# Eight more projections of a two-block transformer kernel in three reduced-precision products instead of one float32 product

## The chip, the cores and the metric

The kernel runs on one core of one Trainium2 chip. The metric is the device time of one execution in microseconds (us). The engines that matter are PE (TensorE, the matmuls), DVE (VectorE), ACT (ScalarE), POOL (GpSimd) and SP, whose queue issues the loads of the weights.

## The reference, cut to what matters

Two networks run one after the other. The first, which the change touches, has two blocks (i = 0 and 1) on 256 tokens of width 1024. All data are float32.

```python
for i in range(DEPTH):
    y = swiglu(x, ffn_w_gate[i, 0], ffn_w_up[i, 0], ffn_w_down[i, 0])
    x = layer_norm(ALPHA * x + 0.5 * y, ln_g[i, 0], ln_b[i, 0])
    y = mixer_ab(x, ...) if i % 2 == 0 else mixer_c(x, ...)    # 16 heads of 64, ends in o @ w_out
    x = layer_norm(ALPHA * x + y, ln_g[i, 1], ln_b[i, 1])
    y = memory_attn(x, mem, mem_w_q[i], mem_w_kv[i], mem_w_o[i])
    x = layer_norm(ALPHA * x + y, ln_g[i, 2], ln_b[i, 2])
    y = swiglu(x, ffn_w_gate[i, 1], ffn_w_up[i, 1], ffn_w_down[i, 1])
    x = layer_norm(ALPHA * x + 0.5 * y, ln_g[i, 3], ln_b[i, 3])

def memory_attn(h, mem, w_q, w_kv, w_o):                       # 4 heads of 256, 256 memory rows
    q = (h @ w_q).reshape(...)
    k, v = jnp.split(mem @ w_kv, 2, axis=-1)
    p = softmax(q k^T * MEM_HEAD_DIM ** -0.5)
    return (p v).reshape(B, S, D) @ w_o
```

## The kernel before, in words

Each engine runs one program, in order, and waits on semaphores that other engines raise. `Net` holds what both networks share; `First` holds the first network, with one method for each engine (`tensor`, `scalar`, `vector`, `gpsimd`).

**Weights.** Every weight matrix is streamed from memory in pieces of 128 x 2048 values (1 MB), four to a 1024 x 1024 matrix. `stream_sync` issues them in the order of `net.stream` from SP into a ring of five slots (`weight_ring`), and a piece is issued when the piece five before it has been used by PE (L308 issues weights, L291 other loads).

**Two ways to multiply.** `product` is one place for both. Without halves it is one float32 matmul (L352). With halves, weights and rows each stand as a float32r high part and a float32r low part, and `product` makes three matmuls: low rows by high weights (L349), high rows by low weights (L350), high by high (L351). The trace has two records for each float32 matmul and one for each float32r matmul, so a projection of 1024 x 1024 is 64 or 128 records of L352, or 96 or 192 of L349 to L351 together. `proj_tensor` gives rows in tokens (moving width 512, 32 products), `projT_tensor` gives them transposed (moving width 256, 64 products).

**Making halves.** For weights, `split_scalar` (ACT, L338) waits until the piece has landed and until a slot of the ring of four high halves is free, and copies the piece rounded; `split_vector` (DVE, L344) waits for that and subtracts, over the piece itself. For rows, `halves_copy` does the same from PSUM: ACT takes the high half (L455), then DVE subtracts (L458).

**Before the change** the halves are used in all feed-forward layers, the mixers' input projections and the memory query. Mixer output (`mix_out`), memory keys (`mk`), memory values (`mv`) and memory output (`mo`) of both blocks are float32.

**Attention.** `attn_tensor`, `attn_vector` and `attn_scalar` are three loops over heads, each in the fixed order of its own code. In iteration i PE does scores of head i+1 (L663), the four transposes of the probabilities of head i-1 (L673) and the values of head i-2 (L688). DVE does `top(i)` (in heads with a bias L718, then row maximum L723 and small operations up to L731 or L733), `normalise(i-1)` (to L744), and, where four heads (one in memory attention) are complete, `out(g)`, a copy of PSUM into `oT` (L749). ACT does the exponentials of head i (L777) and the copy of the transposed probabilities of head i-1 (L792). `top(i)` is what the exponentials wait for, and `normalise` what the transposes wait for. The mixer of block 0 has 16 heads, of which 8 to 15 have a window bias and a sink; that of block 1 has 16 heads with a bias, which POOL masks (L1280) after loads from memory.

**Around attention** the order of a block is: feed-forward, normalisation, transposes of x, input projections, mixer attention, `mix_out`, `mk`, `mv`, transposes of x, `mq`, memory attention, `mo`, normalisation (`ln_vector`, L822 to L836, first rows 0 to 127, then 128 to 255), transposes of x (L467), feed-forward. The normalisation after `mix_out` runs beside `mk`; that after `mo` has nothing on PE beside its second part.

## Time and profile before

| what | value |
|---|---|
| device time, median of 3 runs | 3536.83 us (3518.06 to 3536.93) |
| the profiled execution's own time | 3532.46 us |
| its span, first to last instruction | 3530.7 us |
| PE busy | 3180.4 us (90%) |
| DVE busy | 1574.4 us (45%) |
| ACT busy | 1041.6 us (30%) |
| mean granted TensorE clock | 0.938 of full |
| loads of block 1's mixer output weights (4 pieces), issue to landing, median | 9.1 us |
| the same for most other 1 MB pieces | 4.9 to 5.3 us |

All rows are from the one profiled execution. A time in front of a row of a timeline is its start in us from the start of the span. The granted clock is a share of TensorE's full clock: 1.00 is 2.4 GHz, 0.50 is 1.2 GHz. A busy time of PE overlaps with that of its neighbours, because matmuls are pipelined; the time of a stage is therefore read from start to start.

### The profile page before, as it was taken

What the parts mean: (1) busy time and instruction counts of PE and PEld (TensorE: products, weight loads), DVE (VectorE), ACT (ScalarE), POOL (GpSimd) and SP (SyncE); (2) the same over time, 40 slices, a digit from 0 to 9 for tenths busy, and PEclk for the clock granted to TensorE, in tenths of its full rate; (3) what the DMA queues carried; (4) which work ended last, traced back from release to release, by engine and by line L of the source; (5) the groups of instructions that cost most, each with busy time, mean ns of one, the idle gap of its engine ahead of it and who ended that gap; (6) DMA issues with size and microseconds to landing.
All of it is one profiled execution on the core that took longest, in us unless ns stands there. A gap on an engine that the chain in (4) does not pass through costs nothing.

```text
span 3530.7 us, 33459 instructions
## 1 busy us (share of the span) xinstructions
PE 3180.4 (90%) x14288; PEld 2381.6 (67%) x14288; DVE 1574.4 (45%) x1875; ACT 1041.6 (30%) x1220; POOL 106.7 (3%) x85
## 2 busy tenths in 40 slices
PE   8986999976989999797989799988897999999999
PEld 6873668755774768643774488445843788888887
DVE  4446234433444244426742444257433444444444
ACT  4333124323332234203110243131001343434343
POOL 0001000000011000000000000000000000000000
PEclk9998999987998999898899899997998999999999
DMA  6540435545623445353104255432032455555554
GB/s 249 171 160 11 155 131 191 183 126 148 204 84 119 160 137 181 106 178 114 40 2 156 72 180 178 145 118 73 1 124 69 143 182 183 187 181 191 174 173 149
DMA packets 249105, 487.97 MB, mean 138 GB/s; under 512 B 36318, under 2 KB 67678, under 8 KB 248574
## 3 DMA queue, kind: packets, MB, share of 16 engines
q1 hardware_dynamic: 248576, 482.17, 41.1%
q10 hardware_dynamic: 380, 3.66, 0.4%
q8 instruction: 113, 1.85, 0.2%
q14 instruction: 36, 0.29, 0.0%
HBM read 481.08 MB, written 4.69 MB: 138 GB/s over the span
## 4 chain that ended last, share of the span: by engine, by line
PE 78%; DVE 9%; DMA 5%; ACT 3%; SPq 2%; issue 1%; POOL 1%; ACTq 0%; DVEq 0%; POOLq 0%
PE psum L352 18%; PE psum L349 16%; PE psum L351 16%; PE psum L350 16%; PE psum L1861 2%; SPq L291 2%; PE psum L1937 2%; PE psum L688 2%; PE psum L467 2%; PE psum L663 2%; PE psum L1848 2%; DMA weight_ring<-in_ffn_w_gate 1%; DMA weight_ring<-in_moe_wd 1%; ACT weight_high_halves L338 1%; PE psum L549 1%
## 5 line engine op out<-in xcount | busy, mean ns | idle before, releaser
L344 DVE TENSOR_TENSOR weight_ring_low_halves<-weight_ring,weight_high_halves 128x2048 fp32r<-128x2048 f32 (+1 forms) x346 | 743.3, 2156 | 963.9 <-ACT weight_high_halves L338 963.7
L349 PE MATMUL psum<-weight_high_halves,stage_area_halves 128*128 128x512 f32 (+2 forms) x2616 | 1011.7, 387 | 60.5 <-DVE weight_ring_low_halves L344 55.5
L351 PE MATMUL psum<-weight_high_halves,stage_area_halves 128*128 128x512 f32 (+2 forms) x2616 | 1001.9, 383 | 0.0
L350 PE MATMUL psum<-weight_ring_low_halves,stage_area_halves 128*128 128x512 f32 (+2 forms) x2616 | 1001.8, 383 | 0.0
L338 ACT ACTIVATE weight_high_halves<-weight_ring 128x2048 fp32r<-128x2048 f32 (+1 forms) x346 | 622.4, 1806 | 867.3 <-PE psum L351 399.8
L352 PE MATMUL psum<-weight_ring,stage_area 128*128 128x512 f32 (+2 forms) x1600 | 674.8, 583 | 12.3 <-DMA weight_ring<-in_w_in 7.3
L349 PEld LDWEIGHTS psum<-weight_high_halves,stage_area_halves 128*128 128x128 f32 x2616 | 500.2, 191 | 158.2 <-DVE weight_ring_low_halves L344 54.2
L351 PEld LDWEIGHTS psum<-weight_high_halves,stage_area_halves 128*128 128x128 f32 x2616 | 499.4, 191 | 98.9
L350 PEld LDWEIGHTS psum<-weight_ring_low_halves,stage_area_halves 128*128 128x128 f32 x2616 | 499.2, 191 | 93.9
L352 PEld LDWEIGHTS psum<-weight_ring,stage_area 128*128 128x128 f32 x1600 | 306.0, 193 | 367.8 <-issue 366.0
L448 ACT ACTIVATE stage_area<-psum 128x512 f32<-128x512 f32 (+2 forms) x126 | 71.8, 578 | 656.9 <-PE psum L352 394.3
L455 ACT ACTIVATE stage_area_halves<-psum 128x512 fp32r<-128x512 f32 (+2 forms) x148 | 78.9, 571 | 211.5 <-PE psum L549 129.4
L498 POOL TENSOR_TENSOR small<-small,constants 128x1 f32<-128x1 f32 (+5 forms) x45 | 65.2, 1449 | 2322.2 <-DVE small L831 1292.1
L458 DVE TENSOR_TENSOR stage_area_halves<-psum,stage_area_halves 128x512 fp32r<-128x512 f32 (+2 forms) x148 | 90.5, 650 | 84.1 <-ACT stage_area_halves L455 83.2
L467 PE MATMUL psum<-constants,stage_area 128*128 128x128 f32 x272 | 42.0, 315 | 83.8 <-DVE stage_area L1485 31.7
L663 PE MATMUL psum<-stage_area 64*128 64x256 f32 (+1 forms) x288 | 88.3, 457 | 22.8 <-DVE stage_area L718 14.4
L595 ACT ACTIVATE stage_area<-psum 128x512 f32<-128x512 f32 (+2 forms) x108 | 59.9, 554 | 155.3 <-PE psum L351 155.2
L467 PEld LDWEIGHTS psum<-constants,stage_area 128*128 128x128 f32 x272 | 36.5, 163 | 95.7 <-DVE stage_area L1485 35.0
L663 PEld LDWEIGHTS psum<-stage_area 64*128 64x128 f32 (+1 forms) x288 | 55.5, 220 | 53.9 <-issue 22.2
L688 PE MATMUL psum<-stage_area 128*64 128x256 f32 (+1 forms) x288 | 83.3, 432 | 0.0
L349 PE MATMUL psum<-stage_area_halves,weight_ring_low_halves 128*128 128x256 f32 x256 | 74.4, 291 | 6.2 <-DVE stage_area_halves L458 6.2
L449 DVE COPY stage_area<-psum 128x512 f32<-128x512 f32 (+1 forms) x42 | 28.5, 678 | 115.0 <-PE psum L467 114.4
(244 smaller groups left out, 2298.9 us busy)
## 6 DMA issues: line engine op xcount, KB each, us to landing
weight_ring<-in_ffn_w_down SPq DMA_DIRECT2D x44, 1024.0 KB, 5.0
weight_ring<-in_ffn_w_gate SPq DMA_DIRECT2D x40, 1024.0 KB, 5.2
weight_ring<-in_ffn_w_up SPq DMA_DIRECT2D x40, 1024.0 KB, 5.2
weight_ring<-in_moe_wd SPq DMA_DIRECT2D x40, 1024.0 KB, 4.9
weight_ring<-in_w_in SPq DMA_DIRECT2D x36, 1024.0 KB, 5.2
weight_ring<-in_moe_wg SPq DMA_DIRECT2D x32, 1024.0 KB, 5.2
weight_ring<-in_moe_wu SPq DMA_DIRECT2D x32, 1024.0 KB, 5.2
weight_ring<-in_mem_w_kv SPq DMA_DIRECT2D x16, 1024.0 KB, 5.2
```

The source lines that it names most:

```text
L338: act.raw.activation(self.high_half(name), self.in_slot(name), ACT.Copy).then_inc(*act.mark("high_halves", ("high", name)))
L344: v.raw.tensor_tensor(self.low_half(name), self.in_slot(name), self.high_half(name), ALU.subtract).then_inc(*v.mark("low_halves", ("halves ...
L349: pe.raw.matmul(out, a[1], w[0], start=start, stop=False)
L350: pe.raw.matmul(out, a[0], w[1], start=False, stop=False)
L351: return pe.raw.matmul(out, a[0], w[0], start=False, stop=stop)
L352: return pe.raw.matmul(out, a, w, start=start, stop=stop)
L448: return eng.raw.activation(dst, src, ACT.Copy)
L455: eng.raw.activation(dst[0], src, ACT.Copy).then_inc(*eng.mark("high_half_taken", (name, "high")))
L458: eng.raw.tensor_tensor(dst[1], src, dst[0], ALU.subtract).then_inc(*self.drained(eng, bank, full, name))
L467: mm = pe.raw.transpose(self.ps[:, g["bank"], i * P:(i + 1) * P], block, self.ident)
L663: mm = pe.raw.matmul(net.ps[:, bank, m * S:(m + 1) * S], h["q"](j, m), h["k"](j), start=(j == 0), stop=(j == h["nk"] - 1))
L688: mm = pe.raw.matmul(net.ps[p0:p0 + rows, bank, ct * S:(ct + 1) * S], h["v"](part, kt), net.pT[:, i % 2, kt, :], start=(kt == 0), stop=(kt ...
```

## The change

Mixer output, memory keys, memory values and memory output of both blocks are planned with `split=True`, so that each of their 32 pieces gets a high half on ACT and a low half on DVE, and PE makes three matmuls in place of each float32 one. The attention output `oT` is written as two halves (`attn_out`: ACT, then DVE) in place of DVE's single copy. The transposed memory `memT` gets halves in each block after the mixer attention (`mem_halves`: one ACT and one DVE operation of 128 x 2048), in space that the query, the probabilities and their transposes have held until then.

The places in the two engines' orders: the four pieces of `mix_out` are split in iterations 11, 12, 13 and 14 of the mixer attention, on ACT after the copy of the transposed probabilities, on DVE at the iteration's end. The four of `mk` are split after the attention, ahead of the normalisation on DVE. Those of `mv` are split on ACT between the copies of `mk`, on DVE after the normalisation. Two pieces of `mo` are split before the memory attention, the third in its iteration 0, the fourth in iteration 1.

```diff
         self.xT_proj = (self.xT_halves[0], self.halves_part(10240, KT, S))
+        self.oT_halves = self.xT_proj
         self.ffn_hT = (self.halves_part(6144, 4, S), self.halves_part(9216, 4, S))
...
-def attn_vector(net, v, tag, heads, per_group, need_bias=()):
+def attn_out(net, eng, tag, g):
+    src = net.ps[:, 4 + g % 2, :].rearrange("p (a t) -> p a t", a=2)
+    dst = [half[:, 2 * g:2 * g + 2, :] for half in net.oT_halves]
+    net.halves_copy(eng, dst, src, 4 + g % 2, (tag, "values", g), (tag, "oT", g))
+def attn_vector(net, v, tag, heads, per_group, ahead=None):
     n = len(heads)
...
     def out(g):
+        if ahead is not None:
+            return attn_out(net, v, tag, g)
         v.wait_ge(*v.at((tag, "values", g)))
...
-def attn_scalar(net, act, tag, heads):
+        net.split_vector(v, (ahead or {}).get(i, []))
+def attn_scalar(net, act, tag, heads, per_group=4, ahead=None):
     n = len(heads)
...
-    for i in range(n + 1):
+    for i in range(n + (1 if ahead is None else 3)):
         if i < n:
             exps(i)
-        if i >= 1:
+        if 1 <= i <= n:
             turned(i - 1)
+        if ahead is None:
+            continue
+        net.split_scalar(act, ahead.get(i, []))
+        if i >= 3 and (i - 3) % per_group == per_group - 1:
+            attn_out(net, act, tag, (i - 3) // per_group)
...
         self.memT = net.part(18944, KT, S)
+        self.memT_halves = (net.halves_part(2048, KT, S), net.halves_part(8192, KT, S))
         self.mem_tok = net.part(E, MT, D)
...
                 st["ab_in"] = net.plan_proj("ab_in", ins["ab_w_in"][0], blocks(1536), KT, split=True)
-                st["mix_out"] = net.plan_proj("ab_out", ins["ab_w_out"][0], blocks(D), KT)
+                st["mix_out"] = net.plan_proj("ab_out", ins["ab_w_out"][0], blocks(D), KT, split=True)
             else:
...
                 self.load_bias(3)
-                st["mix_out"] = net.plan_proj("c_out", ins["c_w_out"][0], blocks(D), KT)
+                st["mix_out"] = net.plan_proj("c_out", ins["c_w_out"][0], blocks(D), KT, split=True)
             wkv = ins["mem_w_kv"][i]
-            st["mk"] = net.plan_proj(f"mem{i}_k", wkv[:, 0:D], blocks(D), KT)
-            st["mv"] = net.plan_proj(f"mem{i}_v", wkv[:, D:2 * D], blocks(D), KT)
+            st["mk"] = net.plan_proj(f"mem{i}_k", wkv[:, 0:D], blocks(D), KT, split=True)
+            st["mv"] = net.plan_proj(f"mem{i}_v", wkv[:, D:2 * D], blocks(D), KT, split=True)
             self.load_norm(4 * i + 2)
             st["mq"] = net.plan_proj(f"mem{i}_q", ins["mem_w_q"][i], blocks(D), KT, split=True)
-            st["mo"] = net.plan_proj(f"mem{i}_o", ins["mem_w_o"][i], blocks(D), KT)
+            st["mo"] = net.plan_proj(f"mem{i}_o", ins["mem_w_o"][i], blocks(D), KT, split=True)
             self.load_norm(4 * i + 3)
...
         net = self.net
-        oT = lambda k, m: net.oT[:, k, m * P:(m + 1) * P]
+        oT = lambda k, m: pick(net.oT_halves, k, m)
+        memT = lambda k, m: pick(self.memT_halves, k, m)
+        memT_all = lambda k: (self.memT_halves[0][:, k, :], self.memT_halves[1][:, k, :])
         xT = lambda k, m: pick(net.xT_proj, k, m)
...
-            net.projT_tensor(pe, st["mk"], lambda k: self.memT[:, k, :], range(4),
-                             [("memT", m, kg) for m in range(MT) for kg in (0, 4)])
-            net.proj_tensor(pe, st["mv"], lambda k, m: self.memT[:, k, m * P:(m + 1) * P], rot)
+            net.projT_tensor(pe, st["mk"], memT_all, range(4), [("memT_halves", i)])
+            net.proj_tensor(pe, st["mv"], memT, rot)
             net.turn_tensor(pe, self.x_turn(n + 2))
...
+    def mem_halves(self, eng, i, tag, heads):
+        high, low = self.memT_halves
+        if eng.name == "scalar":
+            eng.wait_ge(*eng.at(*[("memT", m, kg) for m in range(MT) for kg in (0, 4)], (tag, "oT", heads // 4 - 2),
+                                (tag, "pT", heads - 1), (tag, "values", heads // 4 - 1)))
+            eng.raw.activation(high, self.memT, ACT.Copy).then_inc(*eng.mark("memory_high_half", ("memT_high", i)))
+        else:
+            eng.wait_ge(*eng.at(("memT_high", i)))
+            eng.raw.tensor_tensor(low, self.memT, high, ALU.subtract).then_inc(*eng.mark("memory_halves", ("memT_halves", i)))
...
                 net.turn_copy(act, self.ab_turn())
-                attn_scalar(net, act, "ab", self.ab_heads())
+                tag, heads = "ab", self.ab_heads()
             else:
...
                 net.proj_copy(act, st["c_v"], rot, self.v_take)
-                attn_scalar(net, act, "c", self.c_heads())
-            net.projT_copy(act, st["mk"], range(4), net.kT, ["scalar"])
+                tag, heads = "c", self.c_heads()
+            out, mk, mv, mo = (st[name]["pieces"] for name in ("mix_out", "mk", "mv", "mo"))
+            attn_scalar(net, act, tag, heads, 4, {11 + j: [out[j]] for j in range(4)})
+            self.mem_halves(act, i, tag, len(heads))
+            net.split_scalar(act, mk)
+            for half in range(2):
+                net.projT_copy(act, st["mk"], range(4), net.kT, ["scalar"], range(2 * half, 2 * half + 2))
+                net.split_scalar(act, mv[2 * half:2 * half + 2])
             net.proj_copy(act, st["mv"], rot, self.v_take, [0])
...
             residual_scalar(net, act, n + 2)
-            net.projT_copy(act, st["mq"], range(4), net.qT, ["scalar"])
-            attn_scalar(net, act, f"mem{i}", self.mem_heads())
+            for half in range(2):
+                net.projT_copy(act, st["mq"], range(4), net.qT, ["scalar"], range(2 * half, 2 * half + 2))
+                net.split_scalar(act, mo[:2] if half == 0 else [])
+            attn_scalar(net, act, f"mem{i}", self.mem_heads(), 1, {0: mo[2:3], 1: mo[3:]})
             net.split_scalar(act, st["ffn1"]["gate_up"][0][:2])
...
                 net.turn_copy(v, self.ab_turn())
-                attn_vector(net, v, "ab", self.ab_heads(), 4)
+                tag, heads = "ab", self.ab_heads()
             else:
                 net.split_vector(v, st["c_k"]["pieces"] + st["c_v"]["pieces"])
-                attn_vector(net, v, "c", self.c_heads(), 4)
+                tag, heads = "c", self.c_heads()
+            out, mk, mv, mo = (st[name]["pieces"] for name in ("mix_out", "mk", "mv", "mo"))
+            attn_vector(net, v, tag, heads, 4, {11 + j: [out[j]] for j in range(4)})
+            self.mem_halves(v, i, tag, len(heads))
+            net.split_vector(v, mk)
             ln_vector(net, v, n + 1, 1.0, self.y_names(st["mix_out"]["tag"]))
+            net.split_vector(v, mv)
             net.split_vector(v, st["mq"]["pieces"][:2])
...
             net.split_vector(v, st["mq"]["pieces"][2:])
-            attn_vector(net, v, f"mem{i}", self.mem_heads(), 1)
+            net.split_vector(v, mo[:2])
+            attn_vector(net, v, f"mem{i}", self.mem_heads(), 1, {0: mo[2:3], 1: mo[3:]})
             net.split_vector(v, st["ffn1"]["gate_up"][0][:2])
...
             net.turn_copy(v, self.x_turn(n + 3))
```

## Rows read from the trace of the kernel before

**Rows 1.** The page: the chain that ended last, by engine.

```profile
PE 78%; DVE 9%; DMA 5%; ACT 3%; SPq 2%; issue 1%; POOL 1%; ACTq 0%; DVEq 0%; POOLq 0%
```

**Rows 2.** Busy time by stage: three outputs together, memory keys, query, c values, two attentions.

```profile
core 0: us, PE busy (x) PEld busy (x) DVE busy (x) ACT busy (x) POOL busy (x), PEclk, DMA share, GB/s
343.90:426.60 82.70, 82.70 (x258) 48.73 (x259) 15.53 (x18) 7.77 (x9) 3.04 (x2) 1.00 0.44 147
371.50:399.10 27.60, 27.60 (x130) 24.29 (x129) 5.52 (x8) 1.79 (x3) 1.52 (x1) 1.00 0.36 129
431.00:455.20 24.20, 24.01 (x191) 23.81 (x190) 4.49 (x2) 5.67 (x8) 0.00 (x0) 0.93 0.26 92
1030.90:1053.20 22.30, 22.30 (x99) 18.00 (x97) 4.59 (x2) 6.49 (x7) 0.00 (x0) 1.00 0.16 48
290.10:343.80 53.70, 46.21 (x192) 26.65 (x192) 37.14 (x116) 27.71 (x89) 0.00 (x0) 0.90 0.00 1
455.80:473.00 17.20, 16.07 (x80) 13.53 (x81) 9.04 (x25) 8.06 (x21) 0.00 (x0) 1.00 0.51 183
```

**Rows 3.** Groups by line and shape: the weight halves and the low half of rows.

```profile
L338 ACT ACTIVATE weight_high_halves<-weight_ring 128x2048 fp32r<-128x2048 f32 x285 | 544.8, 1919 | 695.9 <-PE psum L351 282.5 <-DMA weight_ring<-in_ffn_w_gate 154.4 <-DMA weight_ring<-in_ffn_w_down 67.9
L344 DVE TENSOR_TENSOR weight_ring_low_halves<-weight_ring,weight_high_halves 128x2048 fp32r<-128x2048 f32 x285 | 652.6, 2299 | 819.6 <-ACT weight_high_halves L338 819.5
L458 DVE TENSOR_TENSOR stage_area_halves<-psum,stage_area_halves 128x512 fp32r<-128x512 f32 x122 | 78.5, 682 | 30.3 <-ACT stage_area_halves L455 30.1
```

**Rows 4.** Timeline of block 0, head 10 of the mixer attention (start, us).

```profile
318.65 0.68 DVE L718 SCALAR_TENSOR_TENSOR stage_area<-psum,constants 128x512 f32<-128x512 f32 x1
321.35 0.35 DVE L744 TENSOR_SCALAR stage_area<-stage_area,small 128x256 f32<-128x256 f32 x1
321.76 0.66 PE L673 MATMUL psum<-constants,stage_area 128*128 128x128 f32 x4 [0.25 <-DVE stage_area L744]
322.22 0.68 DVE L718 SCALAR_TENSOR_TENSOR stage_area<-psum,constants 128x512 f32<-128x512 f32 x1
322.45 0.60 ACT L792 ACTIVATE stage_area<-psum 128x512 f32<-128x512 f32 x1 [0.44 <-PE psum L673]
```

**Rows 5.** Timeline of block 1, mixer attention, heads 10 to 15 and its end.

```profile
1090.52 2.48 SPq L308 DMA_DIRECT2D weight_ring<-in_c_w_out  x4
1098.67 0.60 ACT L792 ACTIVATE stage_area<-psum 128x512 f32<-128x512 f32 x1 [2.77 <-PE psum L673]
1102.57 0.69 DVE L718 SCALAR_TENSOR_TENSOR stage_area<-psum,stage_area 128x512 f32<-128x512 f32 x1 [2.87 <-PE psum L663]
1107.52 0.69 DVE L718 SCALAR_TENSOR_TENSOR stage_area<-psum,stage_area 128x512 f32<-128x512 f32 x1 [2.61 <-PE psum L663]
1111.63 0.69 DVE L718 SCALAR_TENSOR_TENSOR stage_area<-psum,stage_area 128x512 f32<-128x512 f32 x1 [0.47 <-PE psum L663]
1118.07 0.69 DVE L749 COPY stage_area<-psum 128x512 f32<-128x512 f32 x1 [2.85 <-PE psum L688]
```

**Rows 6.** Timeline of the memory attention of block 0.

```profile
458.73 0.47 ACT L777 ACTIVATE stage_area<-psum,small 128x256 f32<-128x256 f32 x1 [3.08 <-DVE small L733]
459.52 0.69 DVE L723 TENSOR_REDUCE small<-psum 128x2 f32<-128x512 f32 x1 [0.83 <-PE psum L663]
461.83 0.69 DVE L723 TENSOR_REDUCE small<-psum 128x2 f32<-128x512 f32 x1 [0.69 <-PE psum L663]
473.01 1.53 PE L352 MATMUL psum<-weight_ring,stage_area 128*128 128x512 f32 x3 [0.83 <-issue]
```

**Rows 7.** Timeline of block 0, end of memory output and its normalisation.

```profile
494.00 1.29 DVE L822 SCALAR_TENSOR_TENSOR x<-psum,scaled_residual 128x512 f32<-128x512 f32 x2 [1.16 <-PE psum L352]
507.10 1.97 PE L467 MATMUL psum<-constants,x 128*128 128x128 f32 x8 [5.50 <-DVE x L836]
```

**Rows 8.** Three stretches of attention, columns as in rows 2; granted clock third from last.

```profile
336.00:339.00 3.00, 1.21 (x7) 0.88 (x8) 2.42 (x12) 1.70 (x6) 0.00 (x0) 1.00 0.00 0
339.00:342.00 3.00, 3.00 (x13) 1.82 (x11) 0.09 (x1) 0.68 (x2) 0.00 (x0) 0.53 0.00 0
1104.00:1107.00 3.00, 3.00 (x8) 1.62 (x6) 0.85 (x4) 1.30 (x5) 0.00 (x0) 0.50 0.76 281
```

## The prediction

> **What bounds the kernel now.** I read the page first. PE is busy for 90% of the span, by its line in the table of times, and stands for 78% of the chain that ended last; DVE has 9% of the chain and ACT 3% [rows 1]. So matmul time taken away should come off the end nearly one for one, unless the stage in which new work is put has another bound. That is why I read the stages next. In the float32 projections PE has no gap: mixer output, memory keys and memory values together take 82.7 us, all of them busy, and memory keys alone 27.6 of 27.6. In attention that is not so. Block 0's mixer attention holds PE for less than its 53.7 us, and DVE and ACT are both well occupied there, with small operations that feed each other [rows 2]. The new splitting work goes into exactly these stages, so the timelines of attention decide, and I read those last.
>
> **What the products save.** A float32 projection takes 82.7 / 3 = 27.6 us. The shape of mixer output, memory values and memory output in three products is measured in the c values projection: 96 matmuls in 22.3 us at full clock. Each such projection saves 27.6 - 22.3 = 5.3 us. Memory keys take 27.6 us too; their shape in halves is the memory query, 24.2 us at a mean clock of 0.93. A stretch at half clock for 7% of twice the time is 3.4 us, which costs 1.7 us, so 22.5 at full clock: 5.1 us saved [rows 2]. Six of the first and two of the second: 6 x 5.3 + 2 x 5.1 = 42.0 us.
>
> The Trainium skill, FP8 and Floating Point Precision, section TensorE Precision Notes, says that true float32 takes four passes, each high or low half with each. The trace agrees with the direction but not with the ratio: three products should then take 3/4 of 27.6, 20.7 us, and the c values took 22.3 [rows 2]. By the page's ratio the saving would be 8 x 6.9 = 55 us.
>
> **What the splitting costs inside mixer attention, block 0.** Making halves of a piece is 1.92 us on ACT and then 2.30 us on DVE [rows 3]. Summed over 34 operations on each engine (32 pieces, 2 memories) that is 65 and 78 us, which both engines have free. But the order matters. In iteration i, DVE does `top(i)`, `normalise(i-1)` and then must wait for the high half that ACT makes in the same iteration; ACT makes it only after the copy of the transposed probabilities of head i-1, and this needs PE's transposes, which need `normalise(i-1)`. Nothing on ACT can run ahead, as its exponentials wait for `top(i)`. So one iteration becomes a chain. In iteration 10 DVE starts at 318.65, ends `normalise` at 321.70, PE's transposes run from 321.76 to 322.42 and ACT's copy from 322.45 to 323.05 [rows 4]. With a split behind it: high half to 324.97, low half to 327.3, and only then the next `top`. That is 8.6 us from start to start. Now it is 3.57 (318.65 to 322.22), of which DVE's copy of `oT`, which this iteration holds, is 0.6; without one it is 2.97. Iterations 11, 12 and 13 each cost 5.6 us more, 16.9 us.
>
> Iteration 14 also holds an `oT` copy. It is 3.57 us now and becomes 8.6 + 0.6 (ACT's `oT` high half behind the split) + 0.6 (DVE's, 0.68 with overlap) = 9.8: 6.2 us more. In iterations 6 and 10, without a split, DVE waits for ACT's high half of `oT`: ACT's copy ends at 323.05, 0.60 for the high half, as for that copy, and 0.68 for the low one [rows 3] give 324.3 where 322.22 stood: 2.1 us each, 4.2. At the attention's end the single copy becomes two operations in a row, 0.65 more. Sum for block 0: 16.9 + 6.2 + 4.2 + 0.65 = 27.9 us.
>
> **Block 1.** Here the iterations are longer, since the clock is at half for much of it: 4.95 us from 1102.57 to 1107.52 [rows 5], with a granted clock of 0.50 [rows 8]. More of the chain is therefore already paid. In iteration 11 ACT's copy ends at 1099.27; high and low half end at 1103.5. From there iterations 12 and 13 take 1.65 (`top`) + 0.65 (`normalise`) + 1.1 to 1.2 (transposes at half clock) + 0.6 + 1.92 + 2.30 = 8.4 us each, and iteration 14 8.4 + 1.2 = 9.6. The first three parts are read off the same kind of rows as in block 0. `top(15)` comes at 1103.5 + 8.4 + 8.4 + 9.6 = 1129.9. Now it comes at 1111.63, 7.2 us before the attention's end (its last copy ends at 1118.76). That is 18.3 us more. Iterations 6 and 10 cost some 2 each as before, the end 0.65: 23 us. The pieces themselves should have landed: they are issued between 1090.5 and 1093.0 [rows 5] and take 9.1 us in the median, so the first may come at 1099.6, beside its turn at 1099.3, and the others well before theirs.
>
> **Memory attention, twice.** Its iterations 0 and 1 each hold a split. ACT's exponentials of head 0 begin at 458.73 and take 1.0; high half to 461.7, low half to 464.0. `top(1)` now starts at 459.52, so it is 4.5 late. Then `normalise(0)` ends at 465.7, transposes 0.6, copy 0.6, high half to 468.9, low half to 471.2, and `top(2)`, now at 461.83, starts 9.3 late [rows 6]. Behind that, each of four heads has its `oT` in two steps: `normalise(3)` comes after the first, the last values wait for a bank that the second frees, and the last pair ends the stage. Walking that through gives 2.0 more: 11.3 us, 22.6 for both.
>
> **What lies outside attention.** The halves of `memT` and of `mk` run beside mixer output, whose pieces free the four high slots at 8.3, 11.1, 19.4 and 22.2 us. The last low half of `mk` ends some 28.8 us after mixer output began, ahead of its use at 33.5. It pushes the normalisation to 28.8 to 41.4 (now 21.0 to 34.0), and behind this the first low halves of `mv` end at 43.7 and 45.9, where PE wants them at 44.8 and 47.6. About 1 us of cover is left; if a load lands later, it is paid one for one. I cost this at nothing.
>
> After memory output the cover is thinner. DVE's normalisation now begins at 494.0 when PE has done the first 128 rows, 21.0 us after memory output began at 473.01; its two parts take 6.2 to 6.5 us each; PE's transposes start at 507.10, 34.1 us after that beginning [rows 6, 7]. With memory output at 22.2 us its first slot is free after 8.4 us, the piece lands 5 us later, its halves end at 17.8, which is later than the 17.0 at which PE is done with those rows, and 17.8 + 6.2 + 6.2 + 0.1 = 30.3 follows. The gain that reaches the transposes is 3.8, not 5.3: 1.5 us lost each time, 3.0 in all.
>
> **The clock.** A gap of 1.9 us on PE in this attention (busy 1.21 of 3 us) is followed by a stretch at 0.53, though PE is busy throughout it; elsewhere it stays at 0.50 for longer [rows 8]. In the changed iterations PE has 2.6 us of work in 8.6, so I expect 1.2 GHz there. What it can cost: 0.45 for each of four transposes in block 0's loop, 1.8; up to 2.5 at its end; up to 4.0 at block 1's end, which now runs at full clock; 1.7 at the start of each mixer output (what the memory query now pays), 3.4; 3 in each memory attention, 6. That is 17.7 at most, and nothing at least. I take half, 9, since the gaps recur but not each need throw the clock.
>
> **Sum.** 27.9 + 23 + 22.6 + 3.0 + 9 = 85.5 us added, 42.0 taken off: 43.5 us slower. On the profiled execution's 3532.5 us that is 3576 us. The median of the runs stands 4.4 us above this execution, so against it the forecast is 1.1% slower.
>
> **Rivals.** *The chain is absorbed, and the kernel ends faster.* If DVE did not have to wait for ACT in the attention iterations (high halves ready before DVE asks), only DVE's own 2.3 us would be added, and in part in its idle time. With the splits wholly hidden the sum is 42.0 - 3.0 - 13.5 (the `oT` pairs: 4.2 + 4 + 1.3 + 4) = 25.5 faster, 3507; with all twelve low halves paid it is 3534, about no change. The point from which it decides is a price of (42.0 - 16.5) / 12 = 2.1 us for each of twelve splits in attention; I read 4.5 to 5.6. For it speaks only that both engines have much free time [rows 2]. Against it stands the order of the code.
>
> *The products gain more.* With the page's 3/4 the saving is 55 and the time 3563. The c values' 22.3 us speak against it.
>
> *The clock stays low for longer.* If each stall leaves PE at half clock, as rows 8 show once, for the whole 17.7, and the projections behind the four attentions lose another 1.7 each, the time is 3576 + 8.7 + 6.8 = 3592.
>
> *The clock does not fall at all:* 3576 - 9 = 3567.
>
> **How the numbers follow.** The chain as worked out, 3562 to 3590: 0.60. The clock stays low for longer: 0.16. The products gain more, or several terms are each somewhat smaller, 3550 to 3565: 0.12. The chain absorbed, 3507 to 3540: 0.12. A measurement of this kernel can tell about 1%, 35 us, from no change. Slower by more than that starts at 3568 on the profiled execution's base: most of the first case and all of the second, 0.63. Within 1%: 0.32. Faster by over 1% needs even the hidden case to gain more than it can: 0.05. The range is 3545 to 3603.
>
> **What would show it.** Right: start to start of L718 in block 0 of some 8.6 us in iterations 11 to 13 against 2.97; DVE's idle time before L344 ending with ACT's L338 inside attention; block 0's mixer attention near 82 us, memory attention near 28 to 31 instead of 17.2; projections at 22.3 to 22.6 us; a granted clock near 0.5 where heads 11 to 15 run. Wrong: if L718 keeps its spacing in those iterations the chain does not exist; if memory keys or mixer output take much over 22.5 us behind their cold start, the halves come late; if PE waits at the start of memory values, the 1 us of cover was not there.

## The result, and the profile after

The changed kernel takes 3575.6 us (median of 4 runs, 3567.91 to 3578.07), the kernel before in the same session 3532.12 us (4 runs, 3518.06 to 3536.93): a ratio of 1.0126, 95% interval 1.0091 to 1.0161. The profiled execution took 3578.07 us with a span of 3576.3 us, 45.6 us more span than before.

The page of the changed kernel, the line of busy times and the chain by engine:

```profile
PE 3155.9 (88%) x14608; PEld 2419.5 (68%) x14608; DVE 1650.2 (46%) x1909; ACT 1113.1 (31%) x1270; POOL 106.7 (3%) x85
...
PE 75%; DVE 11%; DMA 5%; ACT 4%; SPq 2%; issue 2%; POOL 1%; ACTq 0%; DVEq 0%; POOLq 0%
```

PE is busy for 24.5 us less in sum and its share of the chain falls from 78% [rows 1] to 75%; DVE's rises from 9% to 11%, ACT's from 3% to 4%. The products got cheaper and the end moved to the two engines that feed the attentions.

The stretches that answer to [rows 2], in one view of busy time by stretch of the changed kernel: memory keys with mixer output ahead of it (378.0 to 422.7), memory query, the two mixer attentions, the two memory attentions.

```profile
core 0: us, PE busy (x) PEld busy (x) DVE busy (x) ACT busy (x) POOL busy (x), PEclk, DMA share, GB/s
378.00:422.70 44.70, 44.70 (x288) 40.54 (x289) 25.91 (x23) 13.99 (x10) 3.04 (x2) 1.00 0.41 141
449.20:474.30 25.10, 24.34 (x192) 24.15 (x193) 9.08 (x4) 10.06 (x10) 0.00 (x0) 0.93 0.25 91
293.30:377.90 84.60, 56.73 (x192) 31.39 (x193) 46.29 (x120) 37.91 (x98) 0.00 (x0) 0.72 0.00 1
1087.90:1175.30 87.40, 59.56 (x194) 32.30 (x193) 50.76 (x104) 38.77 (x91) 9.31 (x4) 0.69 0.28 84
474.40:505.50 31.10, 21.04 (x81) 16.41 (x81) 13.25 (x26) 12.13 (x26) 0.00 (x0) 0.84 0.28 102
1271.70:1301.50 29.80, 20.09 (x80) 15.09 (x80) 13.25 (x26) 12.13 (x26) 0.00 (x0) 0.89 0.30 106
```

Mixer output and memory keys together are 44.9 us with no gap on PE. Mixer attention of block 0 is 84.6 us long where it was 53.7, and PE is busy for 56.7 of them at a granted clock of 0.72. That is also where the length of the kernel went. Measured from the first matmul of a stage to that of the next, from both timelines:

| stage | before | after | block 1 before | block 1 after |
|---|---|---|---|---|
| mixer attention | 53.73 | 84.68 | 65.52 | 87.43 |
| mixer output | 27.54 | 22.27 | 27.54 | 22.27 |
| memory keys | 27.62 | 22.61 | 27.63 | 22.62 |
| memory values | 27.47 | 22.19 | 27.47 | 22.19 |
| transposes, memory query | 29.31 | 29.33 | 29.32 | 29.32 |
| memory attention | 17.22 | 31.18 | 17.22 | 29.84 |
| memory output to feed-forward | 35.70 | 31.80 | 35.69 | 31.98 |

The two blocks grow by 25.5 and 15.3 us, 40.8 in all. The other 4.8 us of the span lie in stretches whose code did not change: 3.1 ahead of the first attention, 5.9 between the blocks, -4.2 behind them. Over the kernels of this study the stretch between the blocks came out at 534.4 to 550.6 us and the rest behind them at 2239.6 to 2248.4, so these 4.8 us are no effect of the change that could be shown.

The timeline of the changed kernel for iteration 12 of block 0's mixer attention. It answers to [rows 4]; each row is start, duration, engine, line.

```profile
340.13 0.68 DVE L726 SCALAR_TENSOR_TENSOR stage_area<-psum,constants 128x512 f32<-128x512 f32 x1
342.83 0.35 DVE L752 TENSOR_SCALAR stage_area<-stage_area,small 128x256 f32<-128x256 f32 x1
343.23 1.11 PE L674 MATMUL psum<-constants,stage_area 128*128 128x128 f32 x4 [3.88 <-DVE stage_area L752]
344.38 0.60 ACT L803 ACTIVATE stage_area<-psum 128x512 f32<-128x512 f32 x1 [0.90 <-PE psum L674]
344.88 1.90 ACT L339 ACTIVATE weight_high_halves<-weight_ring 128x2048 fp32r<-128x2048 f32 x1
346.81 2.29 DVE L345 TENSOR_TENSOR weight_ring_low_halves<-weight_ring,weight_high_halves 128x2048 fp32r<-128x2048 f32 x1 [3.64 <-ACT weight_high_halves L339]
349.02 0.68 DVE L726 SCALAR_TENSOR_TENSOR stage_area<-psum,constants 128x512 f32<-128x512 f32 x1
```

This is the chain of the prediction, link by link. `normalise` ends at 343.18, PE's transposes follow at 343.23, ACT's copy at 344.38, ACT's high half at 344.88, DVE's low half at 346.81, and the next `top` at 349.02: 8.89 us from start to start, where 2.97 stood. DVE is idle for 3.64 us of it, and the row says for whom. The transposes take 1.11 us, not 0.66 as in [rows 4]: the clock is at half.

The same two places in the memory attention of block 0, against [rows 6]:

```profile
478.17 1.91 ACT L339 ACTIVATE weight_high_halves<-weight_ring 128x2048 fp32r<-128x2048 f32 x1
480.10 2.29 DVE L345 TENSOR_TENSOR weight_ring_low_halves<-weight_ring,weight_high_halves 128x2048 fp32r<-128x2048 f32 x1 [2.89 <-ACT weight_high_halves L339]
482.31 0.68 DVE L731 TENSOR_REDUCE small<-psum 128x2 f32<-128x512 f32 x1
485.62 1.90 ACT L339 ACTIVATE weight_high_halves<-weight_ring 128x2048 fp32r<-128x2048 f32 x1
487.55 2.29 DVE L345 TENSOR_TENSOR weight_ring_low_halves<-weight_ring,weight_high_halves 128x2048 fp32r<-128x2048 f32 x1 [3.63 <-ACT weight_high_halves L339]
489.76 0.68 DVE L731 TENSOR_REDUCE small<-psum 128x2 f32<-128x512 f32 x1
```

`top` of heads 1 and 2 start at 482.31 and 489.76, 7.45 us apart, where 2.31 stood (459.52 to 461.83).

### The profile page after: what moved, and what is told of

The parts are those of the page before. It is cut to its first block, busy times and chain, and to the rows that moved or that the text cites. A ratio compares the mean times of both kernels' runs of the same rounds, so it can differ in the third digit from the quotient of the medians.

```text
span 3576.3 us, 34209 instructions
## 1 busy us (share of the span) xinstructions
PE 3155.9 (88%) x14608; PEld 2419.5 (68%) x14608; DVE 1650.2 (46%) x1909; ACT 1113.1 (31%) x1270; POOL 106.7 (3%) x85
## 4 chain that ended last, share of the span: by engine, by line
PE 75%; DVE 11%; DMA 5%; ACT 4%; SPq 2%; issue 2%; POOL 1%; ACTq 0%; DVEq 0%; POOLq 0%
PE psum L350 17%; PE psum L352 17%; PE psum L351 17%; PE psum L353 11%; PE psum L1904 2%; SPq L292 2%; ACT weight_high_halves L339 2%; DMA weight_ring<-in_ffn_w_gate 2%; PE psum L1980 2%; DVE weight_ring_low_halves L345 2%; PE psum L468 2%; PE psum L1891 1%; PE psum L689 1%; PE psum L674 1%; PE psum L664 1%
## 5 line engine op out<-in xcount | busy, mean ns | idle before, releaser
L345 DVE TENSOR_TENSOR weight_ring_low_halves<-weight_ring,weight_high_halves 128x2048 fp32r<-128x2048 f32 (+2 forms) x378 | 816.5, 2167 | 1001.1 <-ACT weight_high_halves L339 1001.1
L350 PE MATMUL psum<-weight_high_halves,stage_area_halves 128*128 128x512 f32 (+3 forms) x2808 | 1087.0, 387 | 71.1 <-DVE weight_ring_low_halves L345 60.3
L352 PE MATMUL psum<-weight_high_halves,stage_area_halves 128*128 128x512 f32 (+3 forms) x2808 | 1077.4, 384 | 0.0
L351 PE MATMUL psum<-weight_ring_low_halves,stage_area_halves 128*128 128x512 f32 (+3 forms) x2808 | 1076.9, 384 | 0.0
L339 ACT ACTIVATE weight_high_halves<-weight_ring 128x2048 fp32r<-128x2048 f32 (+2 forms) x378 | 683.7, 1815 | 912.3 <-PE psum L352 439.8
L350 PEld LDWEIGHTS psum<-weight_high_halves,stage_area_halves 128*128 128x128 f32 x2808 | 536.0, 191 | 178.6 <-DVE weight_ring_low_halves L345 59.1
L352 PEld LDWEIGHTS psum<-weight_high_halves,stage_area_halves 128*128 128x128 f32 x2808 | 534.9, 190 | 107.2
L353 PE MATMUL psum<-weight_ring,stage_area 128*128 128x512 f32 (+2 forms) x1216 | 507.9, 579 | 8.6 <-DMA weight_ring<-in_w_in 6.5
L353 PEld LDWEIGHTS psum<-weight_ring,stage_area 128*128 128x128 f32 x1216 | 232.9, 194 | 272.7 <-issue 271.1
L468 PE MATMUL psum<-constants,stage_area 128*128 128x128 f32 x272 | 43.9, 325 | 87.1 <-DVE stage_area L1528 31.7
L350 PE MATMUL psum<-stage_area_halves,weight_ring_low_halves 128*128 128x256 f32 x384 | 110.6, 288 | 6.2 <-DVE stage_area_halves L459 6.2
L674 PE MATMUL psum<-constants,stage_area 128*128 128x128 f32 x256 | 53.6, 345 | 70.4 <-DVE stage_area L752 70.2
L352 PE MATMUL psum<-stage_area_halves,weight_high_halves 128*128 128x256 f32 x384 | 110.1, 287 | 0.0
L351 PE MATMUL psum<-stage_area_halves,weight_high_halves 128*128 128x256 f32 x384 | 109.9, 286 | 0.0
```

What stands on the lines that cost most here:

```text
L339: act.raw.activation(self.high_half(name), self.in_slot(name), ACT.Copy).then_inc(*act.mark("high_halves", ("high", name)))
L345: v.raw.tensor_tensor(self.low_half(name), self.in_slot(name), self.high_half(name), ALU.subtract).then_inc(*v.mark("low_halves", ("halves ...
L350: pe.raw.matmul(out, a[1], w[0], start=start, stop=False)
L351: pe.raw.matmul(out, a[0], w[1], start=False, stop=False)
L352: return pe.raw.matmul(out, a[0], w[0], start=False, stop=stop)
L353: return pe.raw.matmul(out, a, w, start=start, stop=stop)
```

## The experiments

All ran in three later sessions (parts 1 to 4, parts 5 to 8, parts 9 and 10), with 18, 13 and 11 runs of the kernel before beside them (medians 3521.87, 3523.06 and 3521.73 us). The expected times stand on the 3532.12 us of the first session, so an expectation is compared here as a ratio to that time, and not as a time. A ratio is to the kernel before; in brackets is its 95% interval.

**Part 1: the wait inside the iteration, in all four attentions.** The edit to the changed kernel:

```diff
-        net.split_vector(v, (ahead or {}).get(i, []))
+        net.split_vector(v, (ahead or {}).get(i - 1, []))
```

> One edit to the changed kernel: VectorE makes each low half of a weight piece one iteration later than ScalarE its high half, in all four attentions. The work is the same, only the wait inside an iteration goes. Theory (the wait in the same iteration is the cost): each mixer iteration with a split shrinks from 8.9 us to some 5.2 (VectorE's own 2.97 + 2.2), the mixer attentions from 84.7 and 87.4 us to about 71 and 75, each memory attention from about 30.5 to about 24; time 3575.6 - 38 = about 3537. Rival (the splitting work itself, or the half clock, is the cost): VectorE and ScalarE have the same work and the clock still falls, so 3565 to 3576.

Measured: 3527.56 us (10 runs), ratio 1.0021 (1.0003 to 1.0039). Mixer attentions 76.4 and 80.3 us, memory attentions 22.7 both. The same operations, on the same engines, and 1% of the kernel's time is back; expected was a ratio of 1.0014. Four starts of `top` from its timeline:

```profile
336.16 0.68 DVE L726 SCALAR_TENSOR_TENSOR stage_area<-psum,constants 128x512 f32<-128x512 f32 x1
341.63 0.68 DVE L726 SCALAR_TENSOR_TENSOR stage_area<-psum,constants 128x512 f32<-128x512 f32 x1
346.79 0.68 DVE L726 SCALAR_TENSOR_TENSOR stage_area<-psum,constants 128x512 f32<-128x512 f32 x1
356.31 0.68 DVE L726 SCALAR_TENSOR_TENSOR stage_area<-psum,constants 128x512 f32<-128x512 f32 x1
```

Iterations 12 and 13 are 5.47 and 5.16 us, as expected. Iteration 14, the last gap, is 9.52 us. DVE there still waits for ACT's high half of an attention output, which stands behind ACT's high half of the fourth piece:

```profile
353.51 0.69 DVE L459 TENSOR_TENSOR stage_area_halves<-psum,stage_area_halves 128x512 fp32r<-128x512 f32 x1 [3.66 <-ACT stage_area_halves L456]
```

I had moved the wait for the weights and left that for the rows. The mixers came out 5 us above the expectation, but iteration 14 is not the main reason, since iteration 11 has lost its low half and fell to 2.97 us. From `top` of head 11 to mixer output, block 0 takes 13.0 us less than in the changed kernel, near the 13.7 expected. The other 4.7 us were lost in iterations 4 to 6, whose code is the same in both kernels and which ran at a lower granted clock here (first the changed kernel, then this one):

```profile
306.90:318.30 11.40, 11.40 (x48) 6.66 (x48) 5.18 (x16) 5.61 (x17) 0.00 (x0) 0.89 0.00 1
304.10:320.30 16.20, 16.20 (x48) 8.88 (x48) 5.25 (x17) 5.62 (x17) 0.00 (x0) 0.61 0.00 1
```

In block 1 it is the same: 13.8 us less from `top` of head 11 on, 6.6 us more ahead of it.

**Part 2: no work in the attentions.** Mixer output, memory output and attention output back in float32, keys and values in halves:

```diff
-st["mix_out"] = net.plan_proj("ab_out", ..., KT, split=True)
+st["mix_out"] = net.plan_proj("ab_out", ..., KT)
...
-st["mo"] = net.plan_proj(f"mem{i}_o", ..., KT, split=True)
+st["mo"] = net.plan_proj(f"mem{i}_o", ..., KT)
...
-attn_vector(net, v, tag, heads, 4, {11 + j: [out[j]] for j in range(4)})
+attn_vector(net, v, tag, heads, 4)
```

and the same on ACT and in the memory attentions.

> The changed kernel with only memory keys and memory values (and the transposed memory) in halves; mixer output, memory output and the attention output are float32 as before, so no attention holds any added work. Theory: all four attentions are back at 53.7, 65.5 and 17.2 us, memory keys stay at 22.6 and values at 22.2 us, nothing is paid, and the time is 3532.1 - 2 x (5.0 + 5.3) = about 3511. Rival (splitting costs something wherever it is done, by slots, loads or a late normalisation): above 3525.

Measured: 3501.88 us (9 runs), ratio 0.9948 (0.9931 to 0.9964), faster than before. Busy time in block 0's mixer attention and in memory keys:

```profile
290.40:345.00 54.60, 47.11 (x192) 27.16 (x193) 37.13 (x116) 28.44 (x90) 0.00 (x0) 0.87 0.00 1
372.20:395.10 22.90, 22.90 (x194) 22.66 (x193) 17.50 (x19) 7.34 (x6) 3.04 (x2) 1.00 0.47 164
```

The attention is back at 54.6 us and memory keys take 22.9 to 23.0, so the 16 pieces that are split beside projections cost nothing that shows. The ratio gives 18 us where 20.6 were expected, within the interval (12.7 to 24.3).

**Part 3: the last two pieces of memory output, split behind the memory attention.**

```diff
-attn_vector(net, v, f"mem{i}", self.mem_heads(), 1, {0: mo[2:3], 1: mo[3:]})
+attn_vector(net, v, f"mem{i}", self.mem_heads(), 1, {})
+net.split_vector(v, mo[2:])
```

and the same on ACT.

> One edit to the changed kernel: the last two pieces of memory output are split after the memory attention, beside the first half of memory output, instead of in its iterations 0 and 1. Theory: two chained splits are worth 9.3 us and about 2 to 3 more of half clock; each memory attention falls from about 30.5 to 19.8 us, which leaves the 2 us or so of the attention output in two steps; time 3575.6 - 21.5 = about 3554. Rival (what makes memory attention slow is the attention output in two steps): it stays above 27 us and the time above 3568.

Measured: 3550.77 us (4 runs), ratio 1.0086 (1.0066 to 1.0106). The memory attention of block 0:

```profile
472.40:491.70 19.30, 16.45 (x80) 13.28 (x80) 8.94 (x24) 9.17 (x25) 0.00 (x0) 1.00 0.44 164
```

From start to start it is 19.47 us. Two chained splits were 10.4 to 11.7 us of each memory attention, and 2.25 us is what the attention output in two steps costs. The two memory attentions are 22.1 us shorter together, as expected, but the ratio is above the expected 1.0062: the mixer attentions, whose code did not change, took 86.1 and 92.3 us here against 84.7 and 87.4.

**Part 4: ACT's work stays, DVE's moves behind the mixer attention.** `attn_vector(..., {})` with `net.split_vector(v, out)` behind it; ACT as in the changed kernel.

> One edit to the changed kernel: in the mixers, ScalarE still makes the high halves of the output weights in iterations 11 to 14, but VectorE makes all four low halves after the attention. Theory (VectorE's in-order wait is the cost, not ScalarE's work): iterations 11 to 13 of block 0 are back near 3.0 to 4.0 us, bounded by ScalarE's or VectorE's own work; the mixer attentions up to the first matmul of the output are 65 to 70 us with about 2.3 us of waiting for the first low half; time 3575.6 - 35 = about 3541. Rival (ScalarE's 1.9 us in each iteration delays the exponentials): iterations of 5 us and more, time above 3555.

Measured: 3540.8 us (4 runs), ratio 1.0063 (1.004 to 1.0087). Mixer attentions 71.3 and 71.4 us, mixer output 25.0: the 2.7 us above 22.3 are the wait for the low halves, which falls inside it rather than ahead. Attention and mixer output together are 23.9 us shorter in the two blocks, where 35 were expected, and the ratio is above the expected 1.0025, next to the 1.0065 (3555 us) from which the rival was to count. By the iterations the rival does not hold. Iterations 11 to 13 of block 0 take 2.96, 4.49 and 4.24 us, the last two at a granted clock of 0.61. Without any work on ACT, in part 6, iterations 12 and 13 take 5.19 and 4.95 us at 0.50. With it, but at full clock, those of block 1 take 2.54, 2.90 and 2.65 us here. So ACT's 1.9 us show no price of their own, which leaves DVE's wait and its own 2.3 us.

**Part 5: the wait alone.** DVE waits for the high half where it did, and makes the low halves later:

```diff
-        net.split_vector(v, (ahead or {}).get(i, []))
+        for name in (ahead or {}).get(i, []):
+            v.wait_ge(*v.at(("high", name)))
...
+            net.split_vector(v, out)
```

In the memory attentions the pieces are split in place, as before this edit.

> In the mixers, VectorE still waits for the high half in iterations 11 to 14, as in the changed kernel, but makes the low halves only after the attention. Against the run that had no wait either (mixer attentions of 71.3 and 71.4 us, mixer output 25.0) this adds the wait alone; against the changed kernel it takes the 2.3 us of work alone away. Theory (wait 3.6 us and work 2.3 us of the 5.9 us of each iteration): start to start 6.6 us in iterations 11 to 13, mixer attention of block 0 about 76 us, time 3575.6 - 12.6 = about 3563. Rival (the wait is covered, ScalarE's work alone sets the iteration): as without the wait, 71 us and 3541.

Measured: 3561.8 us (4 runs), ratio 1.0114 (1.0097 to 1.013). Starts of `top` in iterations 12 and 13:

```profile
336.92 0.69 DVE L726 SCALAR_TENSOR_TENSOR stage_area<-psum,constants 128x512 f32<-128x512 f32 x1 [3.17 <-ACT weight_high_halves L339]
343.61 0.69 DVE L726 SCALAR_TENSOR_TENSOR stage_area<-psum,constants 128x512 f32<-128x512 f32 x1 [3.63 <-ACT weight_high_halves L339]
```

6.69 us from start to start, with 3.63 us of waiting for ACT. So of the 5.92 us that a split added at this clock, 2.20 are DVE's own work and 3.72 the wait. Block 0's attention is 81.7 us against 71.3 in part 4, which has the same work and no wait. Of these 10.4 us, 7.8 stand behind `top` of head 11, where the four waits are; the rest stands ahead of it, in code that is the same. How much of the 7.8 is the lower clock (0.50 in iterations 12 and 13, 0.61 in part 4) stays open. I had expected 76 us and a ratio of 1.0087, and the measured ratio is clear of that: 3.7 of the 5.7 us in block 0 were lost ahead of head 11, where the clock was lower than in the changed kernel, and without reason I had added nothing for the clock.

**Part 6: all pieces of mixer output behind the attention, on both engines.**

> One edit to the changed kernel: both halves of the four mixer output pieces are made after the mixer attention, nothing of them in it. What is left in the attention is its output in two steps (four times) and, at the end, one exposed high and low half, 4.2 us. Theory: mixer attention up to the first matmul of the output 53.7 + 7 + 4.2 = 65 us in block 0 and 76.5 in block 1; time 3575.6 - 30.6 = about 3545, so that keeping the pieces out of the attention altogether still does not pay for the 5.3 us that mixer output saves. Rival (the output in two steps is free): 58 and 70 us, time 3532.

Measured: 3538.49 us (6 runs), ratio 1.0045 (1.0029 to 1.0062). Mixer attentions up to the first matmul of mixer output: 70.9 and 80.4 us, so 5.9 and 3.9 above the expectation; mixer output takes 23.8 and 24.4 us in place of 22.3, since it waits for its halves. The ratio is in line with the expected 1.0036. The timeline of block 0 around iteration 10, which has no split and only the attention output in two steps, and the granted clock at 323 to 326 and at 332 to 335:

```profile
326.20 0.69 DVE L459 TENSOR_TENSOR stage_area_halves<-psum,stage_area_halves 128x512 fp32r<-128x512 f32 x1 [1.87 <-ACT stage_area_halves L456]
329.77 0.68 DVE L726 SCALAR_TENSOR_TENSOR stage_area<-psum,constants 128x512 f32<-128x512 f32 x1
334.96 0.69 DVE L726 SCALAR_TENSOR_TENSOR stage_area<-psum,constants 128x512 f32<-128x512 f32 x1 [2.14 <-PE psum L664]
339.91 0.69 DVE L726 SCALAR_TENSOR_TENSOR stage_area<-psum,constants 128x512 f32<-128x512 f32 x1 [1.89 <-PE psum L664]
```

```profile
323.00:326.00 3.00, 2.75 (x14) 1.57 (x13) 1.23 (x6) 2.10 (x7) 0.00 (x0) 1.00 0.03 5
332.00:335.00 3.00, 3.00 (x8) 1.41 (x7) 0.82 (x4) 1.13 (x5) 0.00 (x0) 0.50 0.00 0
```

DVE waits 1.87 us and takes its low half at 326.20, which makes iteration 10 1.95 us longer than before, and `top` of heads 13 and 14 then come 5.19 and 4.95 us behind the one before, in place of 2.97. The clock is 0.50 there and was 1.00 ahead of it. PE had stood idle for 2.80 us (327.11 to 329.91), and now its own work is the bound: the last two rows wait for PE. Without the 4.2 us for the exposed halves this attention is 13 us longer than before. Of these, 2.7 stand in iterations 1 to 4, ahead of the first attention output, in code that is the same. The two steps of four small outputs thus cost about 10 us with their effect on the clock, not 7. The conclusion of the expectation holds: with the waits left in the rows, mixer output in halves does not pay even with its pieces outside.

**Part 7: PE filled in its waiting time.** Three spare float32 products ahead of the transposes of heads 10 to 15:

```diff
+        if per_group == 4 and i >= 10:
+            for _ in range(3):
+                pe.raw.matmul(net.ps[:, 7, :], net.ident, net.area[:, 4096:4096 + BANK], start=True, stop=True)
         pe.wait_ge(*pe.at((tag, "probs", i)))
```

> The changed kernel with three spare float32 products of 128 x 512 (results unused) before the transposes of heads 10 to 15 of the mixers, in the time in which TensorE waits for VectorE and ScalarE; they fit into the 5.6 us of waiting at either clock. They add no output. Theory (the clock is a minor part, some 3 us in each mixer attention): the granted clock there goes from 0.5 to near 1.0, block 0's attention falls from 84.7 to 81 to 83 us, the time to 3568 to 3573. Rival (half clock is the main cost of the attentions): below 3560.

Measured: 3566.94 us (4 runs), ratio 1.0128 (1.0111 to 1.0145), no different from the changed kernel's 1.0126. The granted clock over 331.3 to 366 was 0.85, higher than in the changed kernel but not near 1.0, and the iterations became shorter:

```profile
331.30:366.00 34.70, 26.23 (x70) 11.79 (x68) 20.59 (x40) 14.56 (x30) 0.00 (x0) 0.85 0.00 0
```

```profile
337.27 0.68 DVE L729 SCALAR_TENSOR_TENSOR stage_area<-psum,constants 128x512 f32<-128x512 f32 x1
345.70 0.68 DVE L729 SCALAR_TENSOR_TENSOR stage_area<-psum,constants 128x512 f32<-128x512 f32 x1
```

8.43 us in place of 8.89. But the attention as a whole took 85.8 us: iterations 11 to 14 gained 1.7 us, and at its end, where PE does not wait, the spare products stand on the path and cost 2.8. A miss as a way to save time. As a measurement it says what the clock is worth inside a split iteration: 0.46 us of 5.92. Part 3 agrees without spare products: its iteration 11, at a granted clock of 0.73, takes 8.43 us, and the next two, at 0.50, 8.89 and 8.90.

**Part 8: the best placement without mixer output.** Part 2 with memory output in halves as in part 3.

> Keys and values in halves as in the run with these two alone, and memory output in halves too, its last two pieces split after the memory attention; mixer output and the mixers' attention output stay float32. Theory: the two mixer attentions are as before the change (53.7 and 65.5 us), each memory attention 19.5 us (17.2 + 2.25 for the attention output in two steps, as measured), memory output to feed-forward 31.8 in place of 35.7; against the run with keys and values alone this gains 2 x (3.9 - 2.25) = 3.3 us, a ratio to before of about 0.994. Rival (memory output in halves is not worth its second step): ratio above 0.996.

Measured: 3495.66 us (6 runs), ratio 0.9917 (0.9898 to 0.9937). Memory attention 19.47 us twice, memory output to feed-forward 31.9 and 31.8. The ratio is better than the expected 0.994, but the stages do not show why: the two blocks take 426.8 us against 428.1 in part 2, 1.3 us less, where the two ratios are 11 us apart. Mixer attentions were 55.1 and 65.8 us here and 54.6 and 64.3 there, with the same code.

**Part 9: the wait for rows in the memory attention.** DVE's low half of an attention output one iteration behind ACT's high half:

```diff
-        if i >= 3 and (i - 3) % per_group == per_group - 1 and i - 3 < n:
-            out((i - 3) // per_group)
+        late = 0 if ahead is None else 1
+        if i >= 3 + late and (i - 3 - late) % per_group == per_group - 1 and i - 3 - late < n:
+            out((i - 3 - late) // per_group)
```

> One edit to the kernel with keys, values and memory output in halves: in the memory attention VectorE takes the low half of an attention output one iteration later than ScalarE its high half. Theory (the wait of one in-order engine on the other in the same iteration is what costs, for rows as for weights): each memory attention falls from 19.47 us by about 1, towards the 17.2 of the single copy plus the 0.65 of the last pair; time 2 us less, ratio to before about 0.991. Rival (the second step costs as such, or the later release of a bank holds TensorE): 19.5 us or more.

Measured: memory attentions 18.34 and 18.35 us, 1.1 less each, as expected. The time, 3494.6 us (6 runs), ratio 0.9922 (0.9906 to 0.9938), can't be told from part 8; 2 us are below what the runs resolve. The stage lengths show the effect, the ratio does not.

**Part 10: the whole change with its waits undone.** The changed kernel with the edits of parts 1, 3 and 9, and mixer output's pieces placed as

```diff
+early = {2: out[:1], 4: out[1:2]} if i == 0 else {11: out[:1], 12: out[1:2]}
-attn_scalar(net, act, tag, heads, 4, {11 + j: [out[j]] for j in range(4)})
+attn_scalar(net, act, tag, heads, 4, early)
+net.split_scalar(act, out[2:])
```

and the same on DVE.

> The whole change (all 32 pieces in halves) with its waits undone: in every attention VectorE's part of a pair comes one iteration after ScalarE's; the first two pieces of mixer output are split in iterations 2 and 4 (block 0) and 11 and 12 (block 1), the last two of mixer output and of memory output after their attention. Theory: mixer attentions fall from 84.7 and 87.4 us to within 3 us of before (56 and 69), mixer output stays at 22.3, memory attentions are near 18.7; against the best run so far this gains about 5 us; ratio to before 0.989 to 0.991. Rival (work of this size in a mixer attention costs more than mixer output gains, wait or no wait): ratio 0.994 or more, mixer attentions above 60 and 72 us.

Measured: 3487.2 us (5 runs), ratio 0.9904 (0.9888 to 0.992), the fastest of all and as expected. Block 0's mixer attention and mixer output:

```profile
290.10:344.60 54.50, 45.09 (x192) 25.91 (x192) 41.28 (x118) 34.25 (x96) 0.00 (x0) 0.94 0.00 1
344.70:366.90 22.20, 22.20 (x96) 18.06 (x97) 11.83 (x6) 10.32 (x6) 0.00 (x0) 1.00 0.33 109
```

The attention is 54.6 us, with both halves of two pieces and four outputs in two steps in it, and all 32 pieces are split. Block 1's is 66.4. In the four kernels whose mixer attention was left as before (the kernel before, parts 2, 8 and 9) block 0's took 53.7 to 55.1 us and block 1's 60.2 to 65.8, so what the work in it costs now is within their spread in block 0, and near it in block 1. The kernel beats both others: 1.0% below the one before, 2.2% below the changed one (0.9904 against 1.0126). Against part 8 the gain is not told from nothing by the ratios, whose intervals overlap; by stages it is there (the two blocks take 411.2 us against 426.8). Of these 15.6 us, 10.6 are mixer output's cheaper products and 2.2 the edit of part 9; 3.0 are a shorter stage of transposes and memory query (27.8 against 29.3), whose code is the same and which comes at either length in other kernels too. The edits were made together: no run has the low halves of rows one iteration late without two pieces moved behind the attention, so what each is worth is open.

## Why the prediction was right

The forecast was 3576 us and 43.5 us more than before; measured are 3575.6 us (43.5 us more than before by the medians), and 40.8 us more in the two blocks by their stages. The steps:

- **Products.** 5.3 and 5.1 us saved per projection: measured 5.27, 5.01 and 5.28. The three products take 22.2 to 22.3 us in the shape of mixer output. The four passes that the Trainium skill, FP8 and Floating Point Precision, section TensorE Precision Notes, gives to true float32 had led to an estimate of 20.7 us; the trace does not agree, and by that estimate the forecast would have been 13 us too low.
- **The chain in block 0's mixer attention.** Predicted 5.6 us per iteration and 27.9 in all without the clock; measured 8.89 - 2.97 = 5.92 per iteration and 30.95 in all, of which 2.7 stand in iterations 1 to 4, ahead of any new instruction. That it is a wait and not work is shown by parts 1, 4 and 5: the same work without the wait gives 5.2 to 5.5 us per iteration, the wait without the work 6.69.
- **Block 1.** Predicted 23 plus clock; measured 21.9. The half clock that stands there anyway hides part of the chain, as the step said. Its listed parts add up to 8.2 to 8.3 us for iterations 12 and 13, not to 8.4; measured are 8.17. That the whole came so close is in part luck: the same mixer attention took 92.3 us in part 3, 4.9 more, and in its unchanged form it took 60.2 to 65.8 us.
- **Memory attention.** Predicted 11.3 each without the clock; measured 13.96 and 12.62. Part 3 parts it into 10.4 to 11.7 for the two chained splits and 2.25 for the two-step outputs (predicted 9.3 plus clock, and 2.0).
- **Memory output.** Only 3.8 of 5.3 us were to reach the transposes; 3.9 and 3.7 did. The mechanism shows in the rows that answer to [rows 7]:

```profile
521.17 2.29 DVE L345 TENSOR_TENSOR weight_ring_low_halves<-weight_ring,weight_high_halves 128x2048 fp32r<-128x2048 f32 x1 [2.78 <-ACT weight_high_halves L339]
523.38 1.28 DVE L838 SCALAR_TENSOR_TENSOR x<-psum,scaled_residual 128x512 f32<-128x512 f32 x2
535.68 0.50 PEld L468 LDWEIGHTS psum<-constants,x 128*128 128x128 f32 x3 [5.22 <-DVE x L852]
```

DVE's normalisation now starts the moment its second low half is done (523.38, 17.9 us after memory output began at 505.50), and not when PE is done with the first rows.

- **The clock.** This term was the least known: up to 17.7, taken as 9. What is left of the attentions' growth after the other terms is 79.4 - 73.5 = 5.9 us: 3.1 in block 0's mixer, -1.1 in block 1's, 4.0 in the two memory attentions. It holds the errors of the chains as well, and the 2.7 us above. The single parts were off. Nothing was paid at the start of mixer output, where I had put 3.4: the granted clock was 0.98 over 374 to 378, after PE had been busy for all of 372 to 374. Inside block 0's loop it was 0.46 per iteration, as taken. The clock where heads 11 to 15 run was forecast near 0.5; it was 0.57 to 0.67 per iteration, because it came back to 1.00 twice in between. Part 6 shows an effect that I had not seen in the sum at all: with the two-step output alone the clock fell too, and then PE's own work, 4.95 us per head at half clock, is the bound.
- **The cover of 1 us ahead of memory values** was there: they began on time in both blocks.

The rival that the chain is absorbed fell with the first profile. The rival of a clock that stays low for longer is partly true in mechanism (0.50 over most of 335 to 365) and small in price: 0.46 us in an iteration by part 7, and nothing in the projections behind the mixer attentions. Part of the agreement of 3576 with 3575.6 is luck: the unchanged stretches moved by 4.8 us between the two profiles.

## What to carry to other kernels

Splitting one piece of work over two in-order engines costs little when the second engine takes its part an iteration later, and the whole round trip when it takes it in the same iteration: here about 1% of the kernel for one index (ratio 1.0126 with `i`, 1.0021 with `i - 1`). Before putting work into a loop "because both engines have time", write down, for each engine in its own order, what the new instruction waits for and what stands behind it. And put it where nothing is in turn waiting, if there is such a place: the pieces split beside projections cost nothing that shows (part 2).

## What the runs showed of the hardware

- In these attentions the granted clock fell behind some short stalls of PE and not behind others. In part 6, block 0, it stayed at 1.00 behind a stall of 1.35 us (first two rows), and behind one of 2.80 us it was 0.50 for 12 us, though PE was busy for all of them (next two rows). In part 4 it was 0.50 behind a stall of 1.35 us (last two rows). So the same stall went either way, and no run shows what decides it.

```profile
314.20:315.60 1.40, 0.05 (x1) 0.05 (x1) 1.33 (x6) 0.79 (x3) 0.00 (x0) 1.00 0.00 0
315.60:326.00 10.40, 9.72 (x45) 5.50 (x45) 8.10 (x26) 6.50 (x22) 0.00 (x0) 1.00 0.01 2
327.10:330.00 2.90, 0.10 (x2) 0.09 (x2) 2.69 (x10) 1.03 (x5) 0.00 (x0) 0.79 0.00 0
330.00:342.00 12.00, 12.00 (x31) 6.64 (x32) 7.41 (x24) 4.32 (x15) 0.00 (x0) 0.50 0.00 0
313.90:315.40 1.50, 0.15 (x2) 0.08 (x2) 1.43 (x6) 0.81 (x3) 0.00 (x0) 1.00 0.00 0
316.40:323.10 6.70, 6.70 (x17) 3.51 (x16) 4.35 (x16) 3.18 (x12) 0.00 (x0) 0.50 0.01 1
```

- PE being busy does not bring the clock back at once: in the kernel before it stayed at 0.50 from 1098 to 1110 us with PE busy throughout. Attention in block 0 is PE-bound at 4.95 us a head at half clock and DVE-bound at 2.97 at full clock. So a small stall can cost more behind it than in it: in part 6, 2.0 us in iteration 10 and 4.2 in iterations 12 and 13.
- The fall did not last into what follows: mixer output ran at full clock from its first microsecond in the changed kernel, 22.27 us in both blocks.
